# A state-space layer, a mixture of experts and four attention layers: small transfers read one block later, the pass count read before the loops, token places computed ahead of the gates, one ring load behind a wait

## The chip, the cores and the metric

The kernel runs on one core of one Trainium2 chip. The metric is the device time of one execution in microseconds, the median over several runs. A profiled execution of the same program gives the trace; its times are used to see where the time goes.

## The reference

All tensors are f32, with 256 tokens of width 1024. A first block (one hybrid state-space mixer, then a hierarchical mixture of experts) is followed by a final norm and by four mixer layers (fox, gla, gdn, fox), each with a residual. Cut to what matters here:

```
x = x + hybrid_mixer(rmsnorm(x))            # w_in: 1024 x 5648 columns used in 11 blocks of 512, and 16 columns for dt
dt = softplus(dt_raw + dt_bias);  a = -exp(a_log);  decays from cumsum(dt * a)
y = ssd_chunked_scan(...) + d_skip * xh
x = x + hierarchical_moe(rmsnorm(x)):
    group = argmax(4 group logits); 2 experts of 8 in the group; gates = g_w * softmax(top 2)
    each token goes to 2 of 32 experts: (silu(x @ w_gate[e]) * (x @ w_up[e])) @ w_down[e], times its gate
x = rmsnorm(x, final_norm)
for layer in 0..3: x = x + mixer(rms_norm(x))   # fox, gla, gdn, fox
```

The expert weights are 32 x (1024 x 512 x 3) f32, 201 MB; all of them are read.

## The kernel before, in words

Each engine has its own list of instructions, written by hand, and they meet at semaphores. Nothing is planned by a program; the order in a list is the order of the source.

**Weights.** SP issues all large loads. They go into a ring of four slots of 2 MB, each load as two halves of 1 MB (`put`, `put_block`). A slot is loaded again when its earlier content was used up (`released`). In the mixer layers a block of 512 columns is cut into four units (m = 0 to 3). For each unit ACT makes a rounded copy `w_h` (`high`, L651), DVE the rest `w_l` (`low`, L1138), and TensorE multiplies in three passes of eight matmuls: L2125 (w_h with hnT_h), L2129 (w_h with hnT_l), L2132 (w_l with hnT_h). There are three buffers for parts (`PARTS`), so ACT can split unit u only when unit u - 3 was multiplied. A block's slot is free when DVE has split its last unit.

**First layer ("ssd").** 11 blocks, `project("ssd", first, end)` on TensorE. ACT copies each finished bank (`copy_bank`, bank b is done with unit 2b + 2), DVE convolves (`conv_lin`, with one `low` between two of its steps), ACT applies the Silu (`ssd_tanh`, behind the banks 4, 7 and 10). Eight early small transfers (`early`: w_dt, five columns, dsk twice) are issued on ACT's queue. ACT then waits for all of them, makes two exponentials of 16 and 8 values (L790, L791), and goes on to the splits. TensorE multiplies the 16 columns of dt (`small_full`, L2055) behind block 0. DVE computes the arguments of the softplus behind it, ACT `softplus_row` behind bank 1, DVE the rest and the running sums; TensorE turns them behind block 2. Behind block 5 SP issues eleven late small loads (`late`).

**Experts.** Once the router's logits are there (`rt_done`), DVE ranks them, writes a mask (`rt_mask`), TensorE sums the mask into places (five matmuls, L2366, L2367, L2368, L2370, then `rt_rank`). DVE waits for ACT's exponentials, computes the gates in six operations, then the places (L1579, L1581), and selects the tokens of the first quad (`select_tokens`, L1589). TensorE gathers them (L2380) and takes the eight quads of four experts each: eight steps for w_gate and w_up (L2393), then the next gather, then four for w_down (L2414), and four scatters (L2425) that DVE adds to x_res (L1629). Each step takes one 2 MB load. The first quad has five extra buffers besides the ring. Behind the loop each engine reads a count of passes (`value_load` of count_i) and enters further passes only if it is over 1 (the If is long, and not entered with these inputs). Then DVE sets `moe_done`, which TensorE (L2082), ACT and the final norm wait for. SP has meanwhile gone on to the blocks of fox0; block 0's load is issued when the slot of the eighth quad's step 8 is free, block 1's when that of step 9 is.

## Time and profile before

| what | us |
|---|---|
| median of 3 runs | 1367.08 (1365.86 to 1375.61) |
| profiled execution, its time | 1373.95 |
| profiled execution, its span | 1372.2 |
| TensorE busy in it | 1140.1 |
| VectorE busy | 635.0 |
| ScalarE busy | 428.8 |

The span runs from the first to the last recorded instruction; the time also holds what lies around it, 1.75 us. Busy shares are means over stages with different limits. Marks on the span: the first layer ends near 253 us, the first expert step begins at 276.1, the last scatter at 733.3, and fox0 begins at 741.7.

### The profile page before, as it was taken

Reading aid. Unit: us, or ns where it says so; the run is one execution under the profiler, and the core shown is the slowest. Engines: PE = TensorE matmul, PEld = TensorE weight load, DVE = VectorE, ACT = ScalarE, POOL = GpSimd, SP = SyncE. Lnnn points to the kernel's source line nnn. Section 1 sums busy time; section 2 is a strip of 40 time slices with the busy share of each in tenths; the row PEclk is TensorE's granted clock in tenths of the full one; section 3 lists DMA queues with packets and bytes.
Section 4 is the critical chain, followed back from the end, with each engine's and each line's share of the span. In section 5 each row is a group of like instructions: output and inputs, shape, how many; then the busy total and the mean of one; then the engine's idle time right before and its main releaser. Section 6 shows DMA issues by size and latency. Waiting matters only on the chain.

```text
span 1372.2 us, 20083 instructions
## 1 busy us (share of the span) xinstructions
PE 1140.1 (83%) x8294; PEld 856.7 (62%) x8294; DVE 635.0 (46%) x1249; ACT 428.8 (31%) x663; POOL 6.1 (0%) x28
## 2 busy tenths in 40 slices
PE   4999989795665756576666999999999989899998
PEld 4899967641221212121124998887679988789887
DVE  3677377620101011010104556767567955664486
ACT  2544334100000000000003534546355652255353
POOL 1000000000000000000000000000000000000000
PEclk9999999797988788897988999999999998899999
DMA  8385234989999999999999743354233520056300
GB/s 281 124 253 180 72 120 154 352 340 410 409 410 410 410 409 410 409 410 410 409 410 312 183 125 123 123 185 147 99 115 132 182 65 3 18 156 181 137 1 31
DMA packets 119655, 312.58 MB, mean 228 GB/s; under 512 B 17059, under 2 KB 17290, under 8 KB 119578
## 3 DMA queue, kind: packets, MB, share of 16 engines
q1 hardware_dynamic: 116864, 310.78, 61.8%
q8 instruction: 56, 0.92, 0.3%
q10 hardware_dynamic: 2714, 0.71, 0.3%
q14 instruction: 21, 0.17, 0.0%
HBM read 310.42 MB, written 1.05 MB: 227 GB/s over the span
## 4 chain that ended last, share of the span: by engine, by line
PE 60%; DMA 28%; DVE 6%; ACT 3%; issue 2%; SPq 1%; ACTq 1%; DVEq 0%
DMA ring<-in_w_up 18%; DMA ring<-in_w_down 9%; PE bank L2125 7%; PE bank L2129 7%; PE bank L2132 7%; PE bank L2150 6%; PE bank L2143 6%; PE bank L2147 5%; PE bank L2393 3%; PE bank L2188 2%; PE bank L2414 2%; DVE w_l L1138 1%; DMA dsk<-in_d_skip 1%; PE bank L2067 1%; PE bank L2207 1%
## 5 line engine op out<-in xcount | busy, mean ns | idle before, releaser
L1138 DVE TENSOR_TENSOR w_l<-ring,w_h 128x1024 fp32r<-128x1024 f32 x204 | 246.6, 1222 | 113.6 <-ACT w_h L651 111.4
L651 ACT ACTIVATE w_h<-ring 128x1024 fp32r<-128x1024 f32 x204 | 214.1, 1057 | 235.0 <-PE bank L2132 129.5
L2393 PE MATMUL bank<-ring,cm 128*32 128x512 f32 x960 | 153.1, 770 | 111.3 <-DMA ring<-in_w_up 57.3
L2393 PEld LDWEIGHTS bank<-ring,cm 128*32 128x32 f32 x960 | 29.8, 126 | 226.8 <-DMA ring<-in_w_up 90.0
L2125 PE MATMUL bank<-hnT_h,w_h 128*128 128x256 f32 x864 | 126.6, 290 | 10.2 <-ACT w_h L651 8.8
L2129 PE MATMUL bank<-hnT_l,w_h 128*128 128x256 f32 x864 | 123.3, 286 | 0.0
L2125 PEld LDWEIGHTS bank<-hnT_h,w_h 128*128 128x128 f32 x864 | 114.0, 195 | 13.8 <-ACT w_h L651 7.5
L2132 PE MATMUL bank<-hnT_h,w_l 128*128 128x256 f32 x864 | 121.9, 284 | 0.0
L2129 PEld LDWEIGHTS bank<-hnT_l,w_h 128*128 128x128 f32 x864 | 113.5, 195 | 0.0
L2132 PEld LDWEIGHTS bank<-hnT_h,w_l 128*128 128x128 f32 x864 | 112.0, 193 | 0.6 <-DVE w_l L1138 0.6
L1614 DVE SCALAR_TENSOR_TENSOR cm<-cm,bank 128x512 f32<-128x512 f32 x8 | 5.5, 688 | 218.4 <-ACT cm L857 218.4
L2143 PE MATMUL bank<-w_h,hnT_h 128*128 128x512 f32 x352 | 102.0, 413 | 2.9 <-DVE cm L1744 1.9
L2414 PE MATMUL bank<-ring,cm 128*32 128x512 f32 x496 | 68.2, 690 | 40.0 <-DMA ring<-in_w_down 35.2
L2150 PE MATMUL bank<-w_l,hnT_h 128*128 128x512 f32 x352 | 96.7, 397 | 3.7 <-DVE w_l L1138 3.7
L2147 PE MATMUL bank<-w_h,hnT_l 128*128 128x512 f32 x352 | 97.7, 401 | 0.0
L857 ACT ACTIVATE cm<-bank 128x512 f32<-128x512 f32 x8 | 4.8, 597 | 264.3 <-PE bank L2393 264.3
L2150 PEld LDWEIGHTS bank<-w_l,hnT_h 128*128 128x128 f32 x352 | 67.5, 193 | 20.0 <-DVE w_l L1138 5.4
L2147 PEld LDWEIGHTS bank<-w_h,hnT_l 128*128 128x128 f32 x352 | 68.4, 194 | 15.2
L2143 PEld LDWEIGHTS bank<-w_h,hnT_h 128*128 128x128 f32 x352 | 65.8, 194 | 18.1 <-DVE cm L1744 2.4
L2414 PEld LDWEIGHTS bank<-ring,cm 128*32 128x32 f32 x496 | 15.4, 122 | 87.5 <-DMA ring<-in_w_down 53.7
L1624 DVE COPY cm<-bank 128x512 f32<-128x512 f32 x8 | 5.5, 691 | 110.6 <-PE bank L2414 110.6
L2380 PEld LDWEIGHTS bank<-cm,hn 128*128 128x128 f32 x288 | 41.6, 230 | 14.1 <-issue 12.4
(417 smaller groups left out, 1344.6 us busy)
## 6 DMA issues: line engine op xcount, KB each, us to landing
ring<-in_w_down SPq DMA_DIRECT2D x62, 1024.0 KB, 15.8
ring<-in_w_gate SPq DMA_DIRECT2D x60, 1024.0 KB, 14.4
ring<-in_w_up SPq DMA_DIRECT2D x60, 1024.0 KB, 15.8
ring<-in_fox_w_in SPq DMA_DIRECT2D x32, 1024.0 KB, 10.7
ring<-in_w_in SPq DMA_DIRECT2D x22, 1024.0 KB, 9.2
ring<-in_gla_w_in SPq DMA_DIRECT2D x12, 1024.0 KB, 6.2
ring<-in_gdn_w_in SPq DMA_DIRECT2D x12, 1024.0 KB, 6.8
ring<-in_w_out SPq DMA_DIRECT2D x8, 1024.0 KB, 6.2
```

The source lines that it names most:

```text
L651: af(part(w_h, u, width), w, ACT.Copy).then_inc(s["high_ready"], 1)
L1138: v.tensor_tensor(part(w_l, u, width), w, part(w_h, u, width).bitcast(F32), ALU.subtract).then_inc(s["low_ready"], 1)
L2125: mm(dst, wh[:, k, :], hnT_h[:, k, :], start=(k == 0), stop=False)
L2129: mm(dst, wh[:, k, :], hnT_l[:, k, :], start=False, stop=False)
L2132: x = mm(dst, wl[:, k, :], hnT_h[:, k, :], start=False, stop=(k == KD - 1))
L2143: mm(dst, hnT_h[:, k, tt], wh[:, j, :], start=(first and k == ends[0]), stop=False)
L2147: mm(dst, hnT_l[:, k, tt], wh[:, j, :], start=False, stop=False)
L2150: x = mm(dst, hnT_h[:, k, tt], wl[:, j, :], start=False, stop=(last and k == ends[1]))
L2188: x = mm(bank[SUM_OF.get(name, SUM_BANK)][:, t * R:(t + 1) * R], sq[:, g % 2, i % 4, t * P:(t + 1) * P], pick(i), start=(i == 0 and t == 0 ...
L2380: x = mm(b4(5 + k // 4)[:, k % 4, :], hn[:, t, own], m_S[:, t, :], start=(t == 0), stop=(t == NT - 1))
L2393: x = mm(bank[a][CAP * e:CAP * (e + 1), :], m_xg[:, 2 * b + r, CAP * e:CAP * (e + 1)], expert_of(w, e)[:, r * FF:(r + 1) * FF], start=(b = ...
L2414: x = mm(bank[3 + n][CAP * e:CAP * (e + 1), :], m_ht[:, c * P + CAP * e:c * P + CAP * (e + 1)], expert_of(w, e)[:, n * BLK:(n + 1) * BLK], ...
```

## The change

Four things are moved or added.

- On ACT, the wait for the early small transfers and the two exponentials go from ahead of the first bank to behind the copy of bank 2; the softplus row goes from behind bank 1 to behind bank 5. On DVE the operations around it go behind the first convolution step (`ssd_steps`), with splits up to unit 14 between argument and result. On TensorE the product for dt goes behind block 1, and the turning of its rows behind block 3.
- The count base `iota` starts at 1 and places are stored as place + 1, with 0 for none, so one subtraction goes. The place operation waits for the first three (of five) matmuls and stands ahead of the gates; these follow the first selection.
- The value load of the pass count goes from behind the loop over quads to ahead of it, on ACT, DVE and TensorE (there between quad 0 and the loop). SP's stays. The If stays where it is.
- SP waits for `moe_done` before it issues the load of fox0's block 1.

```diff
--- before.py
+++ after.py
@@ -506,6 +506,8 @@
                 for i, col in enumerate(col_of[l]):
                     if l == "ssd" and i == SLOTS + 2:
                         load_small(late, s["late_loaded"])
+                    if l == "fox0" and i == 1:
+                        sp.wait_ge(s["moe_done"], 1)
                     put_block(RING_BASE[l] + i, w_of[l], col)
                 groups = wo_of[l].shape[0] // D
                 for i in range(2 * groups):
@@ -575,7 +577,7 @@
                 link(nc.gpsimd.memset(t[:], 0.0))
             for t in (ones, upper, supper, slower, upper64, earlier):
                 link(nc.gpsimd.memset(t[:], 1.0))
-            link(nc.gpsimd.iota(iota_i[:], pattern=[[1, CAP]], base=0, channel_multiplier=0))
+            link(nc.gpsimd.iota(iota_i[:], pattern=[[1, CAP]], base=1, channel_multiplier=0))
             link(nc.gpsimd.tensor_copy(iota[:], iota_i[:]))
 
             def select(a, op, fill, base, pattern, cmul):
@@ -786,9 +788,7 @@
             high(PARTS)
             for dst, src in early:
                 act.dma_start(dst, src, allow_slow_non_contiguous=True).then_inc(s["small_loaded"], 16)
-            act.wait_ge(s["small_loaded"], 16 * N_EARLY)
-            af(ncols[0:16, 0:1], cols[0:16, 0:1], ACT.Exp)
-            af(ncols[0:8, 1:2], cols[0:8, 4:5], ACT.Exp).then_inc(s["cols_ready"], 1)
+
             def ssd_tanh(b):
 
                 if b in SSD_TANH_AFTER:
@@ -798,7 +798,11 @@
 
             for b in range(6):
                 copy_bank("ssd", b, cmf[:, (8 + 2 * b) * T:(10 + 2 * b) * T])
-                if b == 1:
+                if b == 2:
+                    act.wait_ge(s["small_loaded"], 16 * N_EARLY)
+                    af(ncols[0:16, 0:1], cols[0:16, 0:1], ACT.Exp)
+                    af(ncols[0:8, 1:2], cols[0:8, 4:5], ACT.Exp).then_inc(s["cols_ready"], 1)
+                if b == 5:
                     softplus_row(1, rows[:, 1, :], rows[:, 2, :], 16)
                 ssd_tanh(b)
             dst = [28 + 2 * i for i in range(4)] + [36 + 2 * i for i in range(4)] + [20 + 2 * i for i in range(4)] + \
@@ -864,10 +868,10 @@
 
             for name in ("moe_gtc", "moe_htc"):
                 act.sem_inc(s[name], 1)
+            act.wait_ge(s["rt_passes"], 1)
+            passes = act.value_load(count_i[0:1, 0:1], min_val=1, max_val=T // CAP)
             with act.Fori(0, NQ) as q:
                 act_quad(q, s["ring_used"], q * MOE_STEPS)
-            act.wait_ge(s["rt_passes"], 1)
-            passes = act.value_load(count_i[0:1, 0:1], min_val=1, max_val=T // CAP)
             with act.If(passes > 1):
                 with act.Fori(1, passes) as p:
                     with act.Fori(0, NQ) as q:
@@ -1339,12 +1343,9 @@
             v.tensor_tensor(vec[:, FIRST_GAIN:FIRST_GAIN + 8], vec[:, VCOL["norm_w"]:VCOL["norm_w"] + 8],
                             vec[:, VCOL["final_norm"]:VCOL["final_norm"] + 8], ALU.mult).then_inc(s["vec_ready"], 1)
             dve.wait_ge(s["vec_ready"], 2)
-            dve.wait_ge(s["cols_ready"], 1)
-            v.tensor_scalar(ncols[0:16, 0:1], ncols[0:16, 0:1], -1.0, None, ALU.mult)
-            link(v.tensor_scalar(ncols[0:8, 1:2], ncols[0:8, 1:2], -1.0, None, ALU.mult))
-
-
-            def softplus_args(k, R, src, bias, sign, root=None):
+
+
+            def softplus_args(k, R, src, bias, sign, root=None, lows=0):
 
                 if root is not None:
                     link(v.tensor_tensor(rows[0:R, 0], src, root[0:R, :], ALU.mult))
@@ -1352,6 +1353,7 @@
                 link(v.tensor_scalar(rows[0:R, 0], src, bias, sign, ALU.add, ALU.mult))
                 v.scalar_tensor_tensor(out=rows[0:R, 1], in0=rows[0:R, 0], scalar=-1.0, in1=rows[0:R, 0],
                                        op0=ALU.mult, op1=ALU.max).then_inc(s["row_arg"], 1)
+                low(lows)
                 dve.wait_ge(s["row_ln"], k)
 
             def softplus_tail(R, dst):
@@ -1359,19 +1361,24 @@
                 link(v.scalar_tensor_tensor(out=dst, in0=rows[0:R, 0], scalar=0.0, in1=rows[0:R, 2],
                                             op0=ALU.max, op1=ALU.add))
 
-            low(UNITS + PARTS)
-            dve.wait_ge(s["small_done"], 1)
-            dve.wait_ge(s["consts_ready"], 1)
-            softplus_args(1, 16, bank[5][0:16, 0:T], cols[0:16, 1:2], 1.0)
-            softplus_tail(16, rows[0:16, 3])
-            link(v.tensor_scalar(rows[0:16, 1], rows[0:16, 3], ncols[0:16, 0:1], None, ALU.mult))
-            for c in range(NT):
-                x = v.tensor_tensor_scan(fall[0:16, c * P:(c + 1) * P], ones[0:16, :], rows[0:16, 1, c * P:(c + 1) * P],
-                                         0.0, ALU.mult, ALU.add)
-            x.then_inc(s["row_ready"], 1)
-
+            def ssd_steps():
+
+                dve.wait_ge(s["cols_ready"], 1)
+                v.tensor_scalar(ncols[0:16, 0:1], ncols[0:16, 0:1], -1.0, None, ALU.mult)
+                link(v.tensor_scalar(ncols[0:8, 1:2], ncols[0:8, 1:2], -1.0, None, ALU.mult))
+                dve.wait_ge(s["small_done"], 1)
+                dve.wait_ge(s["consts_ready"], 1)
+                softplus_args(1, 16, bank[5][0:16, 0:T], cols[0:16, 1:2], 1.0, None, 3 * UNITS + PARTS)
+                softplus_tail(16, rows[0:16, 3])
+                link(v.tensor_scalar(rows[0:16, 1], rows[0:16, 3], ncols[0:16, 0:1], None, ALU.mult))
+                for c in range(NT):
+                    x = v.tensor_tensor_scan(fall[0:16, c * P:(c + 1) * P], ones[0:16, :], rows[0:16, 1, c * P:(c + 1) * P],
+                                             0.0, ALU.mult, ALU.add)
+                x.then_inc(s["row_ready"], 1)
 
             for k in range(3):
+                if k == 1:
+                    ssd_steps()
                 copied("ssd", 2 * k + 2)
                 turned = bank_units("ssd", SSD_TANH_AFTER[k]) + PARTS
                 conv_lin(k, 8 + 4 * k, VCOL["ssd_conv_w"] + 4 * k, 12, VCOL["ssd_conv_b"] + 4 * k, turned, turned)
@@ -1562,23 +1569,22 @@
             v.tensor_reduce(r_n[:, :, 0:1], gl, AX.X, ALU.max, negate=True)
             v.tensor_reduce(r_n[:, :, 1:2], r_es, AX.X, ALU.max, negate=True).then_inc(s["rt_step"], 1)
             v.memset(r_gate, 0.0)
-            link(v.memset(r_pm, -1.0))
-
-            dve.wait_ge(s["rt_step"], 2)
-            link(v.tensor_tensor(r_ex, r_ex, r_sel, ALU.mult))
-            link(v.tensor_reduce(r_sum[:, :, 0:1], r_ex, AX.X, ALU.add))
-            link(v.tensor_tensor(r_sum[:, :, 1:2], r_sum[:, :, 0:1], r_gs, ALU.mult))
-            link(v.reciprocal(r_sum[:, :, 2:3], r_sum[:, :, 1:2]))
-            link(v.tensor_tensor(r_ex, r_ex, r_sum[:, :, 2:3].to_broadcast([P, NT, EPG]), ALU.mult))
-            link(v.tensor_tensor(r_gate[:, :, 0:NE].rearrange("p t (g e) -> p t g e", g=NG),
-                                 r_ex.unsqueeze(2).to_broadcast(grid), in_group, ALU.mult))
+            link(v.memset(r_pm, 0.0))
             dve.wait_ge(s["rt_mask"], 1)
             dve.wait_ge(s["rt_rank"], 1)
-
-            pm = r_pm[:, :, 0:NE]
-            link(v.scalar_tensor_tensor(out=pm, in0=bank[5][:, P:P + NT * NE].rearrange("p (t e) -> p t e", t=NT),
+            link(v.scalar_tensor_tensor(out=r_pm[:, :, 0:NE], in0=bank[5][:, P:P + NT * NE].rearrange("p (t e) -> p t e", t=NT),
                                         scalar=1.0, in1=r_mask, op0=ALU.add, op1=ALU.mult))
-            link(v.tensor_scalar(pm, pm, -1.0, None, ALU.add))
+
+            def gates():
+
+                dve.wait_ge(s["rt_step"], 2)
+                link(v.tensor_tensor(r_ex, r_ex, r_sel, ALU.mult))
+                link(v.tensor_reduce(r_sum[:, :, 0:1], r_ex, AX.X, ALU.add))
+                link(v.tensor_tensor(r_sum[:, :, 1:2], r_sum[:, :, 0:1], r_gs, ALU.mult))
+                link(v.reciprocal(r_sum[:, :, 2:3], r_sum[:, :, 1:2]))
+                link(v.tensor_tensor(r_ex, r_ex, r_sum[:, :, 2:3].to_broadcast([P, NT, EPG]), ALU.mult))
+                link(v.tensor_tensor(r_gate[:, :, 0:NE].rearrange("p t (g e) -> p t g e", g=NG),
+                                     r_ex.unsqueeze(2).to_broadcast(grid), in_group, ALU.mult))
 
             iota4 = iota[:].unsqueeze(1).to_broadcast([P, QUAD, CAP])
 
@@ -1632,16 +1638,19 @@
             dve.sem_inc(s["moe_h"], 1)
             dve.sem_inc(s["moe_acc"], 1)
             select_tokens(0)
+            gates()
+            dve.wait_ge(s["rt_rank"], 2)
             link(v.tensor_reduce(r_pass[0:1, 0, 0:1], bank[7][0:1, 0:NE], AX.X, ALU.max))
             link(v.tensor_scalar(r_pass[0:1, 1, 0:8], iota[0:1, 0:8], float(CAP), r_pass[0:1, 0, 0:1], ALU.mult, ALU.is_lt))
             link(v.tensor_reduce(r_pass[0:1, 0, 1:2], r_pass[0:1, 1, 0:8], AX.X, ALU.add))
+            link(v.tensor_scalar(r_pass[0:1, 0, 1:2], r_pass[0:1, 0, 1:2], 1.0, None, ALU.add))
             v.tensor_copy(count_i[0:1, 0:1], r_pass[0:1, 0, 1:2]).then_inc(s["rt_passes"], 1)
             dve.wait_ge(s["rt_passes"], 1)
             gathered(0)
+            passes = dve.value_load(count_i[0:1, 0:1], min_val=1, max_val=T // CAP)
             with dve.Fori(0, NQ) as q:
                 dve_quad(q, q, q, s["ring_used"], q * MOE_STEPS)
                 dve_quad_end(q, s["ring_used"], q * MOE_STEPS)
-            passes = dve.value_load(count_i[0:1, 0:1], min_val=1, max_val=T // CAP)
             with dve.If(passes > 1):
                 with dve.Fori(1, passes) as p:
                     for t in range(NT):
@@ -2254,18 +2263,18 @@
             tr(bank[5][:, P:P + NB], cm[0:NB, 1, 0:P], ident[0:NB, 0:NB]).then_inc(s["vec_turned"], 1)
             normed("ssd")
             pe.wait_ge(s["consts_ready"], 1)
-            project("ssd", 0, 1)
+            project("ssd", 0, 2)
             pe.wait_ge(s["small_loaded"], 16 * N_EARLY)
             pe.wait_ge(s["vec_ready"], 2)
             small_full(bank[5][0:16, 0:T], w_dt)
-            project("ssd", 1, 3)
+            project("ssd", 2, 4)
             pe.wait_ge(s["row_ready"], 1)
             for k in range(4):
                 c = k % 2
                 src = rows[0:16, 3, c * P:(c + 1) * P] if k >= 2 else fall[0:16, c * P:(c + 1) * P]
                 x = tr(bank[5][:, T + 16 * k:T + 16 * k + 16], src, ident[0:16, 0:16])
             x.then_inc(s["row_turned"], 1)
-            project("ssd", 3, 10)
+            project("ssd", 4, 10)
             sum_squares("sc", 16, lambda i: colsel64[:, i, :])
             project("ssd", 10, 11, lambda m: m and spread("sc", 16, lambda i: [2 * i, 2 * i + 1], [m - 1] if m < 3 else [2, 3]))
 
@@ -2365,7 +2374,7 @@
             pe.wait_ge(s["rt_mask"], 1)
             mm(bank[5][:, P:P + NE], supper[:], r_mask[:, 0, :], start=True, stop=True)
             mm(bank[5][:, P + NE:P + 2 * NE], ones[:], r_mask[:, 0, :], start=True, stop=False)
-            mm(bank[5][:, P + NE:P + 2 * NE], supper[:], r_mask[:, 1, :], start=False, stop=True)
+            mm(bank[5][:, P + NE:P + 2 * NE], supper[:], r_mask[:, 1, :], start=False, stop=True).then_inc(s["rt_rank"], 1)
             for t in range(NT):
                 x = mm(bank[7][:, 0:NE], ones[:], r_mask[:, t, :], start=(t == 0), stop=(t == 1))
             x.then_inc(s["rt_rank"], 1)
@@ -2441,9 +2450,10 @@
 
             gather(0, 1)
             pe_quad(0, 0, 0, first_slot, s["ring_used"])
+            pe.wait_ge(s["rt_passes"], 1)
+            passes = pe.value_load(count_i[0:1, 0:1], min_val=1, max_val=T // CAP)
             with pe.Fori(1, NQ) as q:
                 pe_quad(q, q, q, ring_slot, s["ring_used"])
-            passes = pe.value_load(count_i[0:1, 0:1], min_val=1, max_val=T // CAP)
             with pe.If(passes > 1):
                 with pe.Fori(1, passes) as p:
                     gather(p * (NQ + 1), p * NQ + 1)
```

## Rows read from the trace of the kernel before

**Rows 1.** The page's 40 slices, what the DMA engines moved.

```profile
GB/s 281 124 253 180 72 120 154 352 340 410 409 410 410 410 409 410 409 410 410 409 410 312 183 125 123 123 185 147 99 115 132 182 65 3 18 156 181 137 1 31
```

**Rows 2.** Timeline: start, us, engine, line, operation, tiles, count [idle before <-releaser], first stage.

```profile
27.58 1.12 PE L2132 MATMUL bank<-hnT_h,w_l 128*128 128x256 f32 x8
34.72 0.20 ACT L790 ACTIVATE ncols<-cols 16x1 f32<-16x1 f32 x1 [15.57 <-DMA dsk<-in_d_skip]
...
36.01 2.08 PE L2125 MATMUL bank<-hnT_h,w_h 128*128 128x256 f32 x8 [7.31 <-ACT w_h L651]
...
40.34 3.63 PE L2055 MATMUL bank<-hnT,w_dt 128*16 128x256 f32 x16
...
55.51 1.12 PE L2125 MATMUL bank<-hnT_h,w_h 128*128 128x256 f32 x8
```

**Rows 3.** Busy time by window: us, five engines (instructions), PEclk, DMA share, GB/s.

```profile
28.00:32.00 4.00, 0.70 (x6) 0.49 (x5) 0.00 (x0) 0.00 (x0) 0.00 (x0) 1.00 0.12 17
66.80:148.00 81.20, 81.20 (x679) 81.04 (x678) 58.48 (x86) 39.36 (x45) 0.00 (x0) 1.00 0.63 206
272.00:276.00 4.00, 4.00 (x26) 3.98 (x25) 0.69 (x1) 0.00 (x0) 0.00 (x0) 0.70 0.20 81
276.00:280.00 4.00, 4.00 (x40) 1.21 (x42) 1.59 (x5) 0.00 (x0) 0.00 (x0) 1.00 0.25 50
722.30:728.90 6.60, 3.22 (x16) 0.60 (x16) 0.00 (x0) 0.00 (x0) 0.00 (x0) 0.76 1.03 369
```

**Rows 4.** Timeline, first stage, one table load.

```profile
63.09 1.28 ACT L797 ACT_TABLE_LOAD   x1
```

**Rows 5.** Timeline, routing and the first two gathers.

```profile
267.37 0.61 PE L2368 MATMUL bank<-cm,supper 128*128 128x32 f32 x2
...
267.80 1.04 PE L2370 MATMUL bank<-cm,ones 128*128 128x32 f32 x4
...
269.06 0.23 DVE L1579 SCALAR_TENSOR_TENSOR cm<-bank,cm 128x64 f32<-128x64 f32 x1
...
269.76 0.49 DVE L1589 TENSOR_TENSOR cm<-iota,cm 128x128 f32<-128x128 f32 x2 [0.24 <-DVE cm L1581]
...
270.31 5.86 PE L2380 MATMUL bank<-cm,hn 128*128 128x128 f32 x32 [1.47 <-DVE cm L1589]
...
289.97 4.04 PE L2380 MATMUL bank<-cm,hn 128*128 128x128 f32 x32
```

**Rows 6.** The chain that ended last, in order of time, at the end of the quads.

```profile
737.18 0.56 DVEq L1644
...
738.04 0.04 DVEq L1644
...
738.80 2.91 issue
```

**Rows 7.** Timeline, quad 1, TensorE waiting for its third step.

```profile
312.50 1.92 PE L2393 MATMUL bank<-ring,cm 128*32 128x512 f32 x16 [1.81 <-DMA ring<-in_w_gate]
```

**Rows 8.** Instruction queue from 739 to 740 us: packets, MB, share.

```profile
q8 instruction: 1, 0.02, 6.1%
```

**Rows 9.** The chain again, last loads of the seventh and eighth quads.

```profile
648.92 17.05 DMA ring<-in_w_down
...
710.36 18.54 DMA ring<-in_w_down
```

**Rows 10.** Timeline, last w_down step of these two quads.

```profile
666.01 1.92 PE L2414 MATMUL bank<-ring,cm 128*32 128x512 f32 x16 [1.90 <-DMA ring<-in_w_down]
...
728.94 3.32 PE L2414 MATMUL bank<-ring,cm 128*32 128x512 f32 x16 [3.40 <-DMA ring<-in_w_down]
```

**Rows 11.** DMA issues from 717 to 721.5 us: count, KB each, median us to landing.

```profile
ring<-in_fox_w_in SPq DMA_DIRECT2D x2, 1024.0 KB, 14.8
...
ring<-in_fox_w_in SPq DMA_DIRECT2D x1, 1024.0 KB, 17.7
```

**Rows 12.** Timeline, ACT's first split of fox0's second block.

```profile
753.52 1.05 ACT L651 ACTIVATE w_h<-ring 128x1024 fp32r<-128x1024 f32 x1
```

## Prediction

> **What bounds the kernel now.** I read the 40 slices of the page first [rows 1]. The reader is to see three stages. Up to about 250 us TensorE is busy and the DMA engines are not; from the tenth to the twenty-first slice (309 to 720 us) the DMA engines run at a constant 409 to 410 GB/s, and TensorE waits for them; from then on TensorE leads again. So both kinds of edit can count, but only at the right place. Then I went to the timeline at each place that the diff touches, to see which wait ends last there.
>
> At the start, TensorE begins the last pass of unit 2 at 27.58 and then stands still for 7.31 us, for ACT's w_h [rows 2]. ACT itself idled for 15.57 us, waiting for the early small transfers (the last is dsk), before it made the two tiny exponentials at 34.72. All four ring blocks had landed: 17 GB/s moved from 28 to 32 us [rows 3]. So the gap comes from the order of ACT's list, not from missing data. Later in this layer TensorE has no idle time at all, 81.20 us of 81.20, for 679 matmuls, and 24 of them make a unit: 2.87 us each.
>
> In the routing, the DMA engines have run out of free buffers: 81 and 50 GB/s from 272 to 280 [rows 3]. The stream for the experts restarts when TensorE finishes its first expert step and frees a slot. From there it is limited by its own rate until the last w_down has landed. A microsecond won before 276 us therefore moves the whole of the stream, and the end, by a microsecond; one won on any engine inside the quads is worth nothing.
>
> **Part 1, the small transfers behind block 1.** After the change ACT no longer stops before unit 3. Its w_h for unit 3 waits for unit 0 only (done at about 22.7) and takes about 1.06 us; DVE follows with 1.2 us, done at about 25.2, so unit 3 starts where unit 2 ends, at 28.5 (a pass is a third of a unit, 0.96 us). Units 3 to 7 end at 28.5 + 5 x 2.88 = 42.9. The dt product takes 3.6 us [rows 2] and ends at 46.5, where unit 8 starts. Before, unit 8 starts at 55.5. **Gain 8.9 us**: 7.3 of idle time, 1.4 because unit 3 came slowly after the gap (36.01 to 40.34 is 4.3 us, not 2.9), the rest is rounding.
>
> What is moved with it: ring block 4's load is issued when unit 3 is split, near 25 us and not at 37.3, so 2 MB now run beside the small transfers; block 5's near 37 and not 51; the 11 late small loads behind it on SP's queue (27 us of issuing) end near 65 and not 79, and block 6 behind them is earlier, too. The unknown cost is when the early small ones land. Lower bound 34.7 as now; upper bound 34.7 plus the 5 us that 2 MB take, 39.7, or about 45 with block 5 as well. TensorE needs them at 42.9 and ACT at 38.9, where the next w_h (units 9, 10) is needed on TensorE only at 49.4. I take 37, cost zero; the high end costs 2 us.
>
> The softplus row moves to bank 5. DVE now reaches it after unit 12's split, near 55 us; ACT serves it near 60 with two table loads in place of one (1.28 us each [rows 4]), as the Silu behind bank 4 changed the table. By my count row_ln comes at 63.2, DVE's four operations behind it (1.5 us) end at 64.8, and TensorE asks for row_ready at 69.6. The first convolution step of bank pair 1 then starts 8 us later against TensorE than before, and the splits of units 15 to 19 are queued behind it: w_l of 15 is there at 67.4 for a need of 68.7, w_h of 19 at 78.4 for 78.7. It fits with 0.3 to 1.3 us to spare. If that cover is gone, it is 0 to 2 us of TensorE idle time; I take 0.
>
> **Part 2, places ahead of gates.** Now DVE waits for ACT's exponentials, does six gate operations, then the place operation at 269.06 and a subtraction, and selects at 269.76 [rows 5]. After the change the place operation waits for the third matmul alone (267.37 + 0.61 = 267.98, not the count's end at 268.84). So it starts near 268.0. From it to the select are 0.70 us now, of which the subtraction (one such operation, 0.23 us and a short gap) goes: the select starts at 268.46, **gain 1.3 us** at the gather (270.31 becomes 269.0). A count base of 1 costs nothing. The gates (under the 1.7 us from 267.37 to 269.06) and the pass count (five small operations, about 1 us) now fall beside the gather of 5.86 us, whose first half is needed by DVE only 3.9 us after its start. Bounds: 0.9 (the count's end holds the gather back to 269.4 after all) and 3.1, if the shorter gap brings TensorE's higher clock back earlier: a later gather, at the higher clock throughout, takes 4.04 us, so 1.8 more. I take 1.3.
>
> **Part 3, pass count early.** Behind the last x_res addition DVE's value load takes from 737.18 to 738.08, 0.9 us on the path to moe_done at 738.80 [rows 6]. It goes ahead of the loop, behind gathered(0), where its next result is needed 12 us later. TensorE's own load also lies between the last scatter and L2082, which sits idle 4.75 us; I have no row for its length and take DVE's 0.9. So both shift by 0.9: **gain 0.9 us**. The 2.91 us of issue behind moe_done remain: the If with its long body stays. Bounds 0 (TensorE is bound by something else there) and 2.0. What it costs at the new place: TensorE loads the value between quad 0 and quad 1, 0.9 us, which is hidden by the 1.81 us for which it waits for DMA at 312.50 [rows 7]; the slots freed 0.9 us later don't starve the DMA engines, which then have three blocks in flight. ACT's load lies ahead of its first tanh at 288.39, far from any path.
>
> Here the Trainium skill, "Runtime: NRT & Kernel Launch", section Instruction fetch mechanics, says that a taken branch out of the fetched window forces a fetch by DMA before execution goes on. The trace agrees: one packet of the instruction queue runs between 739 and 740 us [rows 8]. By that rule the 2.91 us stay, as I have them.
>
> **Part 4, block 1 of fox0 held until moe_done.** SP is the only one behind this wait; nothing but ring loads is queued there. The last w_down landed 18.54 us after its issue, that of an earlier quad 17.05: 1.49 us later, and the last 16 matmuls then ran 3.32 us and not 1.92, another 1.4 [rows 9, 10]. In that stretch the engines moved 369 GB/s, not 410 [rows 3]. If block 1 were to blame, holding it gives 2.9 us. But block 0, issued first (717.76) and not held, landed near 733 (14.8 us), and block 1's first half, issued at 719.47, at 737 (17.7 us) [rows 11]: they arrive in the order of issue, one at a time. So block 1 was hardly moving when w_down was late, by 728.9. I take 0; ends 0 and 2.9. What it costs, in the times of before: issued at about 738 (now 719.5), block 1 lands about 7 us later, at 745; ACT first splits it at 753.52 [rows 12]. 8 us of cover remain, and blocks 2 and 3 follow 5 to 7 us apart for needs 11 us apart.
>
> The Trainium skill, "DMA: Bandwidth & Descriptors", section Queues, rings and completion order, says that each DMA engine takes the descriptors of one queue in ring order. By that rule a transfer issued later can't go ahead, and the hold is worth nothing; the order of landings above agrees.
>
> **Sum.** 8.9 + 1.3 + 0.9 + 0 = 11.1 us. The profiled execution has a span of 1372.2 and a time of 1373.95, 6.9 us above the median of the runs, 1367.08; it would come down to 1362.9. Off the median: 1367.1 - 11.1 = **1356.0 us**, 0.8% faster. From no change a measurement of this kernel can tell about 1%, 13.7 us, so the forecast lies just inside it.
>
> **Rivals.**
> Rival A, block 0 and 1 together had slowed the last w_down. For it: the lower rate and the 1.49 us. Against: the order of landings. It gives 2.9 more, or with the earlier clock in the gather (1.8) 4.7 more: 1353.1 to 1351.3, faster by over 1%.
> Rival B, the layer's start gives less: the small transfers land after 43 us or the splits of units 15 to 19 come late. For it: the margins of 0.3 to 1.3 us, and 2 MB beside the small packets. It takes 2 to 5 us: 1358 to 1361.
> Rival C, the stream of experts is bound by its bytes from earlier on, and its end stays. For it: twelve slices at 410 GB/s. Against: 81 and 50 GB/s from 272 to 280. Only part 3 would be left: 1366.2. It is also the form in which the change does not do what it says.
> Rival D, slower: the early small transfers starve beside blocks 4 and 5 and the late small ones. TensorE would wait for them at the dt product from 42.9 on. The price is the landing time less 42.9; with part 2 and 3 in hand it decides from a landing at 54.0 on, and at 62 it is 8 us slower, 1375. Against: 34.7 now, with three of the four ring blocks beside them up to 29 us.
>
> **How the numbers follow.** Forecast (1354 to 1358) 0.42; rival A 0.27; rival B 0.21; C 0.05; D 0.05. The range leaves out C and D and half of the tail of A: 1350 to 1361.5. Faster by over 1% (below 1353.4): most of A and a tenth of the forecast, 0.30. Slower by over 1%: 0.03. Within: 0.67.
>
> **What would show it.** Right: no idle time of TensorE between units 2 and 8; the dt product near 43; the gather 10.2 us earlier and the first quad's first step as well; steady 61.4 us per quad; L2082 11.1 us earlier. Wrong: TensorE idle for w_l between 60 and 85 us, a dt product that waits for a DMA, or a last w_down that lands 17.05 us after its issue.

## The result

The changed kernel took 1351.15 us, the median of 4 runs (1348.07 to 1353.42), against 1366.47 for the kernel before on the same chip (4 runs, 1365.72 to 1375.61): a ratio of 0.9873, interval [0.9842, 0.9903], or 17.4 us of 1367; the two medians are 15.3 us apart, as one run of before (1375.61) weighs on the ratio. A second comparison gave 0.988 [0.985, 0.9909], 16.4 us (medians 1352.43 and 1367.05, 14.6 us apart). The prediction was 1356.0, within 1% of before. The time lies inside the range that it gave, but the gain is 1.1 to 1.3%, not 0.8%: some 4 to 6 us more than the 11.1 that were forecast, which lie outside both intervals (13.3 to 21.6 and 12.4 to 20.5 us).

What the 40 slices of the page show after the change, to be held against [rows 1]:

```profile
GB/s 289 135 248 187 125 63 183 350 401 409 409 410 410 409 410 409 410 410 409 410 409 248 255 133 117 125 188 157 92 113 138 183 68 3 13 157 178 153 1 32
```

Twelve slices at 409 to 410 GB/s, as before; the ninth, in which that stretch begins, has 401 now and had 340. It is as many slices long as before and begins earlier. So the start's gain was carried through the expert stream, which is what rival C denied.

The first stage in the timeline (start, us, engine, line, tiles, count, idle time before it), for [rows 2], and a window of busy times (us, then PE, PEld, DVE, ACT, POOL, granted clock, DMA share, GB/s) for the longest of [rows 3]:

```profile
39.66 0.18 ACT L803 ACTIVATE ncols<-cols 16x1 f32<-16x1 f32 x1
...
43.80 3.63 PE L2064 MATMUL bank<-hnT,w_dt 128*16 128x256 f32 x16
...
47.36 1.22 PE L2134 MATMUL bank<-hnT_h,w_h 128*128 128x256 f32 x8
```

```profile
47.36:142.00 94.64, 94.64 (x789) 94.39 (x788) 64.39 (x99) 51.15 (x59) 0.00 (x0) 1.00 0.57 182
```

The reader is to see no bracket behind any of these lines. ACT finds the small transfers at 39.66 without a wait, the product for dt begins at 43.80 and unit 8 at 47.36; it was 55.51. From there to 142 us TensorE is busy all the time, so the splits of units 15 to 19 came in time.

The routing in the timeline, for [rows 5]:

```profile
258.03 0.61 PE L2377 MATMUL bank<-cm,supper 128*128 128x32 f32 x2
...
258.46 1.04 PE L2379 MATMUL bank<-cm,ones 128*128 128x32 f32 x4
...
258.78 0.23 DVE L1575 SCALAR_TENSOR_TENSOR cm<-bank,cm 128x64 f32<-128x64 f32 x1 [1.37 <-PE bank L2377]
259.25 0.49 DVE L1595 TENSOR_TENSOR cm<-iota,cm 128x128 f32<-128x128 f32 x2 [0.24 <-DVE cm L1575]
...
259.79 5.30 PE L2389 MATMUL bank<-cm,hn 128*128 128x128 f32 x32 [0.29 <-DVE cm L1595]
```

The place operation starts while the count's matmuls (258.46 to 259.50) still run, and is followed by the selection at once.

The end of the experts in the chain, for [rows 6, 9], then the same place in the timeline, for [rows 10]:

```profile
700.54 16.32 DMA ring<-in_w_down
716.87 0.04 issue
716.91 3.51 PE bank L2423 x16
...
721.37 3.71 PE bank L2434 x8
...
725.34 0.55 issue
725.89 0.06 DVE heads L1665
725.95 2.30 DVE w_l L1142 x2
```

```profile
711.78 1.93 PE L2423 MATMUL bank<-ring,cm 128*32 128x512 f32 x16 [2.94 <-DMA ring<-in_w_down]
716.91 3.45 PE L2423 MATMUL bank<-ring,cm 128*32 128x512 f32 x16 [3.20 <-DMA ring<-in_w_down]
721.37 3.70 PE L2434 MATMUL bank<-cm 128*128 128x512 f32 x8 [1.01 <-DVE cm L1630]
726.00 1.97 PE L2091 MATMUL bank<-ident,x_res 128*128 128x128 f32 x16 [0.93 <-DVE heads L1665]
```

This is where the forecast is beaten in the trace. Before, a row of 2.91 us of issue stood behind moe_done [rows 6]. Now there is none: TensorE's first matmul (726.00) comes 0.05 us behind the end of the operation that sets moe_done (725.95). The chain goes on through DVE's splits instead.

How much earlier the changed kernel reaches a mark, in two pairs of profiled executions (start in the one less start in the other, us). Pair 1 is the two profiles of the result. Pair 2 was taken later, both kernels on one chip, and is the one called before_again and after_again below:

```
mark                                     pair 1   pair 2
TensorE at 103 us of before                8.1      8.2
router's product                           7.2      6.2
first mask matmul                          9.3      4.1
first gather                              10.5      5.2
last w_down but one, first matmul         10.5      6.0
last scatter, start                       11.9      7.2
first matmul behind moe_done              15.7     12.4
at 950 us of before                       15.1     12.3
end of the span                           20.5     12.2
```

The pairs agree on what the change does (start 8.1 and 8.2; mask to gather 1.2 each; scatter to first matmul 3.8 and 5.2, of which 1.6 are a slower scatter of before_again) and differ where the clock differs. From the router's product to the first mask matmul there are 10.2 us in one execution of each kernel and 8.1 in the other. The windows of the product (us, busy times, then the granted clock, DMA share, GB/s) show why; the first is of after, the second of after_again:

```profile
249.10:253.10 4.00, 3.99 (x32) 3.85 (x32) 3.04 (x12) 0.00 (x0) 0.00 (x0) 0.91 0.97 371
```

```profile
248.48:254.60 6.12, 6.12 (x32) 5.98 (x32) 3.03 (x12) 0.00 (x0) 0.00 (x0) 0.58 1.00 385
```

The same 32 matmuls at 0.91, mostly the upper of the two levels, or 0.58, mostly the lower. Before has the slow form in its first profile and the fast one in its second, so those 2.1 us belong to neither kernel. The 5.4 us that pair 1 adds behind 950 us look like the same kind: pair 2 adds none, and they arise where before had a clock of 0.78 and 0.83 (1160 to 1200 us) and after 0.87 and 0.89 (1145 to 1180 us).

### The profile page after: what moved, and what is told of

The parts are those of the page before. It is cut to its first block, busy times and chain, and to the rows that moved or that the text cites. A ratio compares the mean times of both kernels' runs of the same rounds, so it can differ in the third digit from the quotient of the medians.

```text
span 1351.7 us, 20085 instructions
## 1 busy us (share of the span) xinstructions
PE 1119.6 (83%) x8294; PEld 844.0 (62%) x8294; DVE 634.6 (47%) x1249; ACT 431.3 (32%) x665; POOL 6.1 (0%) x28
## 4 chain that ended last, share of the span: by engine, by line
PE 63%; DMA 25%; DVE 6%; ACT 3%; issue 1%; SPq 1%; ACTq 0%; DVEq 0%
DMA ring<-in_w_up 17%; DMA ring<-in_w_down 8%; PE bank L2134 8%; PE bank L2138 8%; PE bank L2141 8%; PE bank L2152 6%; PE bank L2159 6%; PE bank L2156 5%; PE bank L2402 5%; PE bank L2423 2%; PE bank L2197 2%; DVE w_l L1142 1%; PE bank L2076 1%; PE bank L2216 1%; PE bank L2389 1%
## 5 line engine op out<-in xcount | busy, mean ns | idle before, releaser
L2402 PE MATMUL bank<-ring,cm 128*32 128x512 f32 x960 | 147.0, 744 | 113.4 <-DMA ring<-in_w_up 68.0
L2423 PE MATMUL bank<-ring,cm 128*32 128x512 f32 x496 | 68.4, 690 | 47.9 <-DMA ring<-in_w_down 43.1
L2389 PEld LDWEIGHTS bank<-cm,hn 128*128 128x128 f32 x288 | 35.9, 203 | 11.6 <-issue 11.1
```

Of the source, the lines that this page charges most:

```text
L2389: x = mm(b4(5 + k // 4)[:, k % 4, :], hn[:, t, own], m_S[:, t, :], start=(t == 0), stop=(t == NT - 1))
L2402: x = mm(bank[a][CAP * e:CAP * (e + 1), :], m_xg[:, 2 * b + r, CAP * e:CAP * (e + 1)], expert_of(w, e)[:, r * FF:(r + 1) * FF], start=(b = ...
L2423: x = mm(bank[3 + n][CAP * e:CAP * (e + 1), :], m_ht[:, c * P + CAP * e:c * P + CAP * (e + 1)], expert_of(w, e)[:, n * BLK:(n + 1) * BLK], ...
```

## The parts alone

Four kernels, each the kernel before with one part of the diff (project 0-2 stands for the call that multiplies blocks 0 and 1):

```
p1_start   ACT's wait and exponentials behind bank 2, softplus row behind bank 5, ssd_steps, project 0-2, 2-4, 4-10
p2_places  iota base 1, places ahead of gates(), the third matmul sets rt_rank, count behind select_tokens(0)
p3_count   passes = value_load(...) ahead of the loops on ACT, DVE and TensorE
p4_hold    if l == "fox0" and i == 1: sp.wait_ge(s["moe_done"], 1)
```

> The kernel before with part 1 alone: the small transfers' exponentials behind the copy of block 1, the softplus row at bank 5, the dt product behind unit 7. My theory: the gain is all in the first layer. Unit 8 starts near 47.4 and not 55.5 (8.1 us), and the gather, the expert stream and moe_done are all earlier by that same 8 to 9 us, up to 2 us more where TensorE's higher clock comes back at another place before the router. Time 8 to 10 us under before. Rival: the stream of experts is bound by its bytes, and the eight microseconds are lost between 276 and 720 us; then moe_done and the time stay within 2 us of before. The last w_down lands some 18.5 us after its issue, as before, since the hold isn't there, and TensorE still stands some 4.7 us behind the last scatter.

> The kernel before with part 2 alone: the places ahead of the gates, the pass count behind the first selection. My theory: the gather starts 1.2 us earlier than before against the mask matmul, the gather itself and all behind it move by the same, and the time is 1 to 2 us lower, at the edge of what can be told. Rival: the earlier gather also runs at TensorE's higher clock (4.0 us in place of 5.9); then 3 us lower. Nothing changes behind the last scatter: 4.7 us of TensorE without work there, 2.9 of them as issue behind moe_done.

> The kernel before with part 3 alone: ACT, DVE and TensorE each load the pass count ahead of their loops over the quads. Theory as in the prediction: DVE's 0.9 us ahead of moe_done go and the 2.9 us of issue on TensorE behind moe_done stay: 0.9 us lower. Rival, which the trace of the changed kernel suggests: TensorE's own value load and the jump over the If wait behind it were what held TensorE, and with the load early the jump is fetched while DVE adds the last outputs; then the next matmul starts within 1 us of moe_done, and the time is 3.8 us lower. A third theory: the 2.9 us came from the fetch of instructions beside block 1 of the next layer on the DMA engines, so that they stay here, where nothing is held.

> The kernel before with part 4 alone: block 1 of fox0 waits for moe_done. As predicted: no effect, the last w_down lands some 18.5 us after its issue. Rival A of the prediction, smaller: the last w_down lands 1.5 us earlier (within 17.0 us of its issue), and moe_done with it, 1.5 us lower. If the fetch of instructions was delayed by that block, the issue of 2.9 us behind moe_done goes as well: 4.4 us lower. Block 1 lands some 14 us after its issue in each case, near the time when ACT asks for it.

Measured, 12 runs each against 35 of before (median 1367.54):

```
kernel      median    ratio and interval        gain, us
p1_start    1359.72   0.9937 [0.9917, 0.9958]    8.6 (5.7 to 11.4)
p2_places   1365.44   0.9989 [0.9968, 1.0011]    1.5 (-1.5 to 4.4)
p3_count    1368.45   0.9999 [0.9979, 1.0019]    0.1 (-2.6 to 2.9)
p4_hold     1365.15   0.9984 [0.9960, 1.0007]    2.2 (-1.0 to 5.5)
```

Part 1 is worth what was forecast, 8.9, and its gain outlasts the expert stream: rivals B, C and D fall. Part 2 shows in the trace what its time can't tell: mask matmul at 265.01, gather at 267.65, 2.64 us, against 3.82 in before. Of parts 3 and 4 the times say little, but the traces say more. With the hold alone and the value load late, the issue behind moe_done is gone; only DVE's value load, ahead of moe_done, is still there (L1646). In the chain of p4_hold:

```profile
737.35 0.55 DVEq L1646
...
738.89 0.06 DVE heads L1658
738.95 2.30 DVE w_l L1140 x2
```

and in that of p3_count, early load, nothing held:

```profile
735.75 0.55 issue
736.30 0.07 DVE heads L1656
736.37 0.94 issue
```

DVE's 0.9 us are gone there, as forecast, and of the 2.9 us most. But p3_count ran its last scatter in 5.46 us and not 3.70, which by itself hides 1.8 us of whatever TensorE waits for. So it decided nothing yet: at the common length 2.7 us would be left, by an estimate (0.94 + 1.76).

The four gains add up to 12.4 us, with some 6 us of uncertainty. Only that of part 1 is clear of noise.

The traces showed another thing. In each of the four, held or not, the last w_down's matmuls began 5.1 us behind those of the one ahead (before: 722.31 to 728.94, 6.6 us [rows 10]). The trace of the changed kernel alone had suggested that the hold brings this 1.5 us.

## Fetch or value load

```diff
 q_no_hold: the changed kernel, less
-                    if l == "fox0" and i == 1:
-                        sp.wait_ge(s["moe_done"], 1)
 q_pe_late: the changed kernel, and on TensorE alone
-            pe.wait_ge(s["rt_passes"], 1)
-            passes = pe.value_load(...)
             with pe.Fori(1, NQ) as q:
                 pe_quad(q, q, q, ring_slot, s["ring_used"])
+            passes = pe.value_load(...)
```

> The changed kernel once more, on the chip of the three kernels that go with it. The parts alone gave 8.6, 1.5, 0 and 2.2 us off the median, 12.3 in all, where the whole change gave 17. If the parts add up, the ratio to before is 0.991 here; if there is an interaction between them (the start's gain comes back larger where TensorE's clock returns at another place, or the load and the hold need each other), it is again 0.987 or below. TensorE starts within 1 us of moe_done, and the instruction queue's packet behind the last scatter comes within 2 us of that scatter's start.

> The changed kernel without the hold, so block 1 of fox0 is issued right behind block 0, the pass count loaded early. In the parts alone the 2.9 us of issue on TensorE behind moe_done vanished with the hold and a late load, and also with the early load and no hold, but there the last scatter ran 5.5 and not 3.7 us, which may have hidden it. Theory F (the fetch of the instructions behind the jump queues behind block 1's bytes, whatever the load does): 1 to 2.9 us of issue come back here, the instruction packet comes 4 to 6 us behind the scatter's start, and the time is 1 to 3 us over the changed kernel. Theory L (TensorE's late value load was the cause): nothing comes back, within 0.5 us of moe_done. The last w_down lands 16.3 to 17.9 us after its issue in both.

> The changed kernel with TensorE's value load where it was, behind its loop; DVE's and ACT's stay early, the hold stays. Theory F: TensorE still starts about 1 us behind moe_done, since the fetch meets free DMA engines and is over before DVE's last addition; the time is that of the changed kernel. Theory L: issue of about 2 us comes back behind moe_done, 2 us over the changed kernel.

> The kernel before, profiled a second time, to see what of its first profile is the execution's own. In that one the last w_down landed 6.6 us after the one ahead of it, in all four kernels with one part alone 5.1 us. If that 1.5 us belongs to the one execution, it is 5.1 here as well, and the hold has nothing to do with it; if block 1 beside it costs it in this kernel, it is 6.6 again. The issue on TensorE behind moe_done should be 1.9 to 2.9 us. The stretch from 750 to 1372 us should be up to 6 us shorter, as TensorE's clock falls.

Measured (6 runs each, 11 of before, median 1367.05): after_again 1352.43, 0.988 [0.985, 0.9909]; q_no_hold 1356.46, 0.992 [0.9893, 0.9947]; q_pe_late 1355.61, 0.9913 [0.9888, 0.9938]; before_again, one run, 1364.5. The changed kernel's 16.4 us (12.4 to 20.5) can't be told from the 12.4 of the parts, so no interaction is shown.

The chain of q_no_hold has the row again, longer than before, with the load early:

```profile
724.70 0.55 issue
725.25 0.07 DVE heads L1663
725.32 3.13 issue
728.45 0.89 PE bank L2089 x6
```

That of q_pe_late has not. In the timeline TensorE starts 0.06 us behind moe_done, with its load late:

```profile
725.85 0.06 DVE L1665 MEMSET heads<- 128x1 f32 x1
...
725.97 1.97 PE L2091 MATMUL bank<-ident,x_res 128*128 128x128 f32 x16 [0.93 <-DVE heads L1665]
```

So theory L falls as the cause of the stall: where the value is loaded didn't make it. Theory F stands: the jump over the If makes TensorE fetch instructions, and the fetch came late behind the loads of fox0. "Block 1" is short for more than one block here. SP's list is in order, so the wait in front of block 1 holds blocks 2 and 3 as well. In q_no_hold the 1 MB halves of block 1 were issued at 708.1 and 712.6, those of block 2 at 715.4 and 716.5 and the first of block 3 at 721.2, all ahead of the packet. Which of these bytes the fetch waited for isn't shown. Nor does a trace show when the packet was asked for, only when it moved. What the DMA engines moved from 720 to 728 us, in 40 slices, first q_no_hold, then the changed kernel:

```profile
GB/s 379 410 399 358 389 410 389 358 410 389 389 389 389 399 358 379 348 236 225 215 205 184 215 184 215 195 205 205 195 154 256 205 205 225 236 236 287 236 297 256
```

```profile
GB/s 328 174 102 113 92 92 61 51 10 0 0 0 0 82 0 0 0 0 0 0 0 0 0 0 0 0 0 0 0 0 0 0 41 82 20 154 82 92 123 164
```

The lone 82 in the second line, in the slice from 722.6 us, is the packet of the instruction queue (q8), on engines with nothing else to do. In q_no_hold it came at 726.0, behind 3.4 us at some 390 GB/s and 2.6 us at some 200.

before_again answers the other question: its last w_down's matmuls follow 5.1 us behind those ahead (719.87, 725.00), with block 1 in flight. The 6.6 us of the first profile belonged to one execution. As expected, too, it stood still behind moe_done, 2.68 us.

What didn't come out is the time of q_pe_late. Theory F expected that of the changed kernel, but its six runs (1354.50 to 1358.95) all lie above the six of after_again (1346.47 to 1353.52), by 3.2 us in the medians. Up to 950 us its trace runs 0.6 us ahead of after_again and has no stall; then it loses some 7 us in two steps (3.0 near 1000, 4.4 between 1150 and 1200). But this profiled execution is its slowest run, 3.3 us over its median, and of the other five there is no trace. So the late load on TensorE may well cost 3 us, and why stays open. For the same reason the 4.0 us between q_no_hold and after_again are no proof of what the hold is worth: q_pe_late is as slow with the hold and without a stall. That the hold removes the stall is shown by the traces, at the place.

## How much of the hold is needed

```diff
 the changed kernel, its wait replaced
-                        sp.wait_ge(s["moe_done"], 1)
 h_scat
+                        sp.wait_ge(s["moe_scat"], 4 * NQ - 1)
 h_used
+                        sp.wait_ge(s["ring_used"], NQ * MOE_STEPS)
```

h_both is the kernel before with the wait for moe_done at block 0, so that both are held; p34 is the kernel before with parts 3 and 4.

> The changed kernel with the hold ended earlier: block 1 waits for the third matmul of the last scatter (some 2 us ahead of moe_done), which is behind the fetch of TensorE's instructions if that comes 1.1 to 1.5 us after the scatter's start, as with the hold. Theory F: no issue on TensorE behind moe_done, block 1 issued 1.9 us earlier and landed 1.9 us earlier, ACT's wait of 0.9 us for it gone; at most 0.5 us better than the changed kernel, since TensorE didn't wait for that block. Rival (the DMA engines' free time up to moe_done is needed, for ACT's, DVE's and later instruction packets as well): some issue comes back, 1 to 3 us over the changed kernel.

> The changed kernel with the hold ended when TensorE has used the last w_down, 1 us before the scatter starts and 2 us before the instruction packet: the dose between held and not held. Theory F: block 1's 1 MB is queued ahead of the packet, which comes 3 to 6 us behind the scatter's start and not 1.5; 0.5 to 3 us of issue on TensorE behind moe_done. The last w_down lands 5.1 us after the one ahead of it, as in every run since.

> The kernel before with blocks 0 and 1 of fox0 both held until moe_done, for rival A of the prediction: that the two together slow the last w_down of the experts. If they do, it lands up to 1.5 us sooner after the one ahead of it than the 5.1 us that all runs but one show, and TensorE's last 16 matmuls may run at the higher clock (1.9 us). If they don't, 5.1 us again. The instruction packet comes 1 to 2 us behind the scatter's start and no issue is left behind moe_done. Block 0 then lands 10 to 15 us after moe_done and TensorE waits for it, 3 to 8 us, so the time is 0 to 6 us over before.

> The kernel before with parts 3 and 4 together. By the traces so far the two are worth 0.9 us (DVE's value load) and 2.9 us (the instruction fetch no longer behind block 1), so moe_done to TensorE's first matmul is 1.0 us and the time 3.8 us under before, 0.997. If part 3 has a cost that part 3 alone shows (its median was no better than before), only the hold's 2 us are left, 0.9985.

Measured: h_scat 1352.07 (6 runs), 0.9877 [0.9839, 0.9915]; p34 1365.10 (12 runs), 0.9991 [0.9966, 1.0016]; h_used 1358.33 and h_both 1377.69, one run each; 17 runs of before, median 1366.78.

The chain of h_used, whose block 1 is issued just ahead of the fetch, has the longest stall of all:

```profile
723.97 0.55 issue
724.51 0.07 DVE heads L1665
724.59 4.43 issue
729.02 1.55 PE bank L2091 x6
```

In h_scat the block is issued 1.6 us ahead of moe_done but behind the fetch, and there is no stall:

```profile
724.32 0.55 issue
724.87 0.06 DVE heads L1665
724.93 2.30 DVE w_l L1142 x2
```

All fourteen profiles, in us. The packet is that of the instruction queue, found in steps of 0.1 us and counted from the start of the last scatter; the stall lies between the end of the operation that sets moe_done and TensorE's next matmul. "Block 1 ahead" means that it was issued ahead of the packet:

```
kernel        block 1 ahead   TensorE's   scatter   packet   stall   packet to
              of the fetch    load                                    first matmul
before        yes             late        3.70      6.0      2.91    2.4
before_again  yes             late        5.31      7.4      2.68    2.4
p1_start      yes             late        3.69      5.0      1.91    2.4
p2_places     yes             late        3.69      5.1      2.02    2.4
p3_count      yes             early       5.46      4.9      0.94    2.4
q_no_hold     yes             early       3.69      5.3      3.13    2.4
h_used        yes             early       3.70      6.6      4.43    2.4
p4_hold       no              late        3.70      2.1      0.05    -
h_both        no              late        5.43      2.1      0.06    -
q_pe_late     no              late        3.69      2.1      0.06    -
p34           no              early       5.53      1.7      0.05    -
after         no              early       3.70      1.2      0.05    -
after_again   no              early       3.70      1.2      0.05    -
h_scat        no              early       5.32      1.2      0.05    -
```

The last column is the strongest part of it. Whenever TensorE stalled, its first matmul came 2.4 us behind the packet, whatever the stall. The packet is the first behind the scatter's start; in the held kernels a second follows 3.0 to 4.2 us later, and as the changed kernel starts its matmul (726.0) ahead of its second (726.6), the start doesn't need that one. The packet itself comes 1.2 to 2.1 us behind the scatter's start on free engines, and 4.9 to 7.4 with block 1 ahead of it. An early value load on TensorE makes it up to 0.9 us earlier (1.2 against 2.1), and the traces show nothing else that it does there. With 2.1 + 2.4 = 4.5 us the late load just fits ahead of moe_done, which comes 4.6 us behind the scatter's start.

Rival A of the prediction can be closed as well. With both blocks held, the last w_down's matmuls came 5.05 us behind those ahead (722.81, 727.86) and took 3.02 us: neither block had slowed it. h_both paid for it otherwise, and more than expected: its one run is 10.9 us over the median of before, where 0 to 6 were expected. ACT waited 18.46 us for block 0, and TensorE 14.28 us behind it. The second half of that load took

```profile
739.56 10.39 DMA ring<-in_fox_w_in
```

p34's time can't show the 3.8 us expected of it: the interval is 4.7 us faster to 2.2 slower. Its trace gives 3.6 at the place (against before_again 2.6 us behind at the last w_down, 1.0 ahead at the first matmul behind moe_done). h_scat is as fast as the changed kernel. Block 1 came before ACT asked for it (no wait at 736.57, where the changed kernel waited 0.90 us), but TensorE wasn't behind that wait. No kernel here is measurably better than the changed one.

## Why the prediction was wrong, point by point

**Part 1, right.** 8.9 us forecast, 8.6 measured alone, 8.1 to 8.2 in the two pairs of traces at 103 us. The product for dt was put at 42.9 and came at 43.80 in after and 43.97 in after_again, as the first units ran 0.8 us slower there than in before (unit 1's last pass began at 25.48 and not 24.70); in p1_start it came at 42.69. ACT found the small transfers landed at 39.66. The sum's own times, 55.5 less 46.5, make 9.0 and not 8.9. The margins that rival B was made of were enough.

**Part 2, right.** 1.3 forecast for the gather, 1.2 in both pairs of traces. The higher clock that was the upper bound didn't come with it: the gather took 5.30 and 6.37 us in the changed kernel, 5.86 and 6.29 in the kernel before.

**Part 3, DVE's 0.9 us right.** The value load's row is gone from the chain. The step that failed stands behind it: "The 2.91 us of issue behind moe_done remain: the If with its long body stays." The jump and its fetch do remain; the packet is in every trace. The stall isn't their length but what of it reaches beyond moe_done. I had seen the packet at 739 to 740 us [rows 8] and didn't ask why it came 6 us behind the start of the last scatter, the last work of TensorE ahead of the jump. Where nothing was in its way, it came 1.2 to 2.1 us behind it, and the stall was 0.05 us. The rule I cited from the Trainium skill ("Runtime: NRT & Kernel Launch", section Instruction fetch mechanics) is right, but it gives no length and doesn't make the stall a constant.

**Part 4, the missing 2.9 us.** I took 0 and was right on what I looked at: the landing of the last w_down, 5.1 us behind the one ahead with the hold and without. Its 1.49 us in [rows 9, 10] was one execution's own, so was the end of 2.9 built on it. The sign that the prediction named for rival A, a last w_down that lands 17.05 us after its issue, did come (16.32 in after), but it came without the hold too (16.7 in before_again, 16.8 in p3_count). Nor is the other 1.4 us a matter of the loads: the same sixteen matmuls took 1.92 to 3.64 us in the fourteen traces, 1.92 in p1_start with nothing held and 3.64 in p4_hold. Rival A came near the right time by the wrong road, which is luck. What the hold is worth was never in my sum, since I asked only which other transfer of SP's queue it could slow. Another queue uses the same sixteen engines: TensorE's instructions. So the term that the sum put at nothing is the stall. It is 2.9 us in the first profile and 1.9 to 3.1 in the others with this scatter length and without the hold (4.4 in h_used, with its hold ended early). With it the sum is 11.1 + 2.9 = 14.0, and the traces show 15.1 and 12.3 up to 950 us, mean 13.7. The 16 to 17 us of the ratios are within their intervals of it. By the runs, the kernel without the hold took 1356.46 us and with it 1352.43, but q_pe_late shows that such a difference can have another cause.

**The cost of the hold, under-rated.** Block 1 was to land 7 us after its issue, with 8 us of cover. It was issued at 725.97 and landed near 740.0, 14 us; ACT was there first:

```profile
740.07 1.06 ACT L653 ACTIVATE w_h<-ring 128x1024 fp32r<-128x1024 f32 x1 [0.90 <-DMA ring<-in_fox_w_in]
```

```profile
726.00:740.00 14.00, 12.10 (x88) 11.86 (x89) 13.22 (x29) 8.38 (x18) 0.00 (x0) 0.88 0.92 215
```

I had priced 2 MB by the 410 GB/s of the expert stream; in this window (after, last column) the engines moved 215. The hold didn't make that rate: at the same loads, with nothing held, it was 211 in before_again (732 to 736 us) and 207 in q_no_hold (723.6 to 727.0). The cover was gone, yet it cost TensorE nothing: its only pause in there, 1.90 us, is for DVE's hnT_l.

**What is late next.** Where the stall is gone, DVE decides: two splits (2.30 us) and the first hnT_l (1.58) lie behind moe_done, so TensorE's projection can't begin sooner than 3.9 us behind it. It was 6.8 before, so that all of the 2.9 us arrived.

## What to carry to other kernels

Behind a jump, ask when the instructions can be fetched and what is then on the DMA engines, not only what the waiting instruction waits for: a prefetch of 2 MB blocks that nobody needs yet cost 2 to 3 us on the path here, and a wait in SP's list, which cost TensorE nothing, won it back. An "issue" row in the chain is not a fixed price. Follow the packet of the instruction queue, see how far behind the last instruction ahead of the jump it comes, and what else was moved in between. And before a term rests on one interval of one execution (6.6 us where thirteen others have 5.0 to 5.2), look for its like elsewhere.

## What the runs showed of the hardware

- A stalled TensorE issued its first matmul 2.4 us behind the packet of its instruction queue, in seven of seven executions.
- With blocks 1 and 2 of fox0 in SP's queue, the packet of the instruction queue came 3.7 to 5.4 us later than on free engines (4.9, 5.3 and 6.6 us behind the scatter's start against 1.2, in the kernels with an early value load). It was latest in h_used, where four 1 MB halves were issued from 719.0 to 720.6, around the scatter's start at 720.0.
- At the block loads of fox0 the engines moved some 210 GB/s for several us, though they were busy (share 0.98 to 1.00): 211 in before_again and 207 in q_no_hold, where they hadn't paused, and 210 in the changed kernel (733 to 737 us), where they had. The experts' loads ran at 410. Why wasn't tried.
- One and the same stretch, router to mask, takes 8.1 or 10.2 us in one and the same kernel, by the clock that is granted to it. Such steps, 1 to 4 us each, fall at other places in each execution. A dozen runs of p34 couldn't show the 3.6 us that its trace has at the place.
